# Seven-product scheme for the first feed-forward too, with in-place weight sums and quartered conditioning weights, in a one-core decoder step

## What is computed

```
c -> s1, sc1, g1, s2, sc2, g2, s3, sc3, g3 = silu(c) @ w_ada + b_ada      # w_ada: 1024 x 9216
h = x + 0.5 * g1 * swiglu(modulate(x, g_ffn1, s1, sc1), w1_gate, w1_up, w1_down)
n = modulate(h, g_mix, s2, sc2); z = n @ w_in
h = h + g2 * (mix of a convolution branch and a sparse attention branch, from z) @ w_out
h = h + 0.5 * g3 * swiglu(modulate(h, g_ffn2, s3, sc3), w2_gate, w2_up, w2_down)
y = rmsnorm(h, g_final)
def swiglu(h, wg, wu, wd): return (silu(h @ wg) * (h @ wu)) @ wd
```

## Time and profile before

| | us |
|---|---|
| median of 3 runs | 2677.19 |
| lowest and highest | 2675.59, 2679.48 |
| the profiled execution's own time | 2673.52 |
| its span in the trace | 2671.7 |
| PE busy | 2509.7 (94%) |
| POOL busy | 1202.6 (45%) |
| DVE busy | 1401.6 (52%) |
| ACT busy | 605.1 (23%) |

### The profile page before, as it was taken

The page is one execution under the profiler, slowest core; times in us unless marked ns, Lnnn a source line. Parts: engine busy times, 40 slices in busy tenths (PEclk is TensorE's granted clock), DMA queues, the critical chain, the costliest instruction groups (busy, mean ns, idle before and its releaser), DMA issues.

```text
span 2671.7 us, 42548 instructions
## 1 busy us (share of the span) xinstructions
PE 2509.7 (94%) x15750; PEld 2331.9 (87%) x15750; DVE 1401.6 (52%) x2533; ACT 605.1 (23%) x1094; POOL 1202.6 (45%) x862
## 2 busy tenths in 40 slices
PE   4999999999999888899999769999899999999998
PEld 2999999999999766699998436789799999999997
DVE  5333333333333727799998645452574444444444
ACT  3311011110102313312344357410511111111113
POOL 1232323223333325546999020124057777777774
PEclk8999999999999879999999879999999999999999
DMA  8322222222211432231224600234011111111112
GB/s 284 119 72 79 71 79 76 67 77 79 72 50 56 148 82 73 73 105 48 83 86 169 196 7 1 77 117 144 1 41 54 48 47 47 47 47 47 47 48 81
DMA packets 208660, 209.94 MB, mean 79 GB/s; under 512 B 14143, under 2 KB 161715, under 8 KB 207657
## 3 DMA queue, kind: packets, MB, share of 16 engines
q1 hardware_dynamic: 198380, 181.70, 21.8%
q10 hardware_dynamic: 10181, 26.90, 3.1%
HBM read 173.03 MB, written 28.94 MB: 76 GB/s over the span
## 4 chain that ended last, share of the span: by engine, by line
PE 82%; DVE 6%; issue 4%; ACT 3%; SPq 3%; DMA 1%; POOL 1%; ACTq 0%; DVEq 0%; POOLq 0%
PE main L249 16%; PE main L250 16%; PE main L251 16%; PE main L2243 4%; PE main L2244 4%; PE main L2245 4%; PE main L2333 2%; PE main L2334 2%; PE main L2335 2%; SPq L1472 2%; DVE pick L1287 2%; PE main L1692 1%; PE aux L2243 1%; PE aux L2244 1%; PE aux L2245 1%
## 5 line engine op out<-in xcount | busy, mean ns | idle before, releaser
L249 PE MATMUL main<-nhi,whi 128*128 128x352 f32 (+1 forms) x2136 | 698.5, 327 | 15.6 <-DVE nlo L465 14.2
L250 PE MATMUL main<-nlo,whi 128*128 128x352 f32 (+1 forms) x2136 | 688.0, 322 | 0.0
L251 PE MATMUL main<-nhi,wlo 128*128 128x352 f32 (+1 forms) x2136 | 687.6, 322 | 0.0
L236 POOL CAST whi<-raw 128x1024 fp32r<-128x1024 f32 x119 | 127.5, 1071 | 989.1 <-PE main L251 697.0
L249 PEld LDWEIGHTS main<-nhi,whi 128*128 128x128 f32 (+1 forms) x2136 | 402.2, 188 | 45.2 <-issue 32.2
L250 PEld LDWEIGHTS main<-nlo,whi 128*128 128x128 f32 (+1 forms) x2136 | 403.0, 189 | 0.6
L251 PEld LDWEIGHTS main<-nhi,wlo 128*128 128x128 f32 (+1 forms) x2136 | 401.9, 188 | 0.6
L238 POOL TENSOR_TENSOR wlo<-raw,whi 128x1024 fp32r<-128x1024 f32 x119 | 296.7, 2493 | 9.5
L687 DVE TENSOR_TENSOR tmp<-main,tmp 128x352 f32<-128x352 f32 x66 | 34.6, 525 | 395.6 <-PE main L251 394.5
L2170 POOL TENSOR_TENSOR blo<-raw,bhi 128x512 fp32r<-128x512 f32 x152 | 203.6, 1340 | 12.2
L2243 PE MATMUL main<-nhi,bhi 128*128 128x352 f32 x576 | 188.6, 327 | 8.3 <-DVE nlo L465 4.5
(11 more groups left out here) (376 smaller groups left out, 4934.5 us busy)
## 6 DMA issues: line engine op xcount, KB each, us to landing
ada_raw<-in_w_ada SPq DMA_DIRECT2D x18, 2048.0 KB, 9.0
raw<-in_w_gate SPq DMA_DIRECT2D x44, 512.0 KB, 3.9
raw<-in_w_up SPq DMA_DIRECT2D x44, 512.0 KB, 3.8
raw<-in_w_down SPq DMA_DIRECT2D x44, 512.0 KB, 3.6
raw<-in_w_in SPq DMA_DIRECT2D x40, 512.0 KB, 3.8
gate_d<-zraw ACTq DMA_DIRECT2D x16, 528.0 KB, 2.7
gates<-gate_d SPq DMA_DIRECT2D x16, 528.0 KB, 4.8
zsw<-zraw ACTq DMA_DIRECT2D x42, 132.0 KB, 2.5
```

Of the source, the lines that this page charges most:

```text
L249: pe.matmul(bank, w_hi[:, w], hi(c), start=(i == 0), stop=False)
L250: pe.matmul(bank, w_hi[:, w], lo(c), start=False, stop=False)
L251: last = pe.matmul(bank, w_lo[:, w], hi(c), start=False, stop=(i == n - 1))
```

## The change

- Feed-forward 1 is done by the same function as feed-forward 2 (ffn, called twice, with a set of semaphore bases each: Signals). Its plain version is gone.
- The four weight sums of a matrix are made in place in the raw tiles (add), so wsum is gone. A raw tile is held until its last sum: tiles 3 and 5 of a step are loaded when the fourth sum of matrix 0 or 1 is set, a count called wsum_set.
- Blocks, units, bank order and DVE's combinations come in another order, and the tile of the second half (sub 1) is loaded first.
- A w_ada tile is loaded and multiplied in quarters of 128 columns (load_ada_part, pe_ada_part), through one buffer ada_part of 512 KB. SP issues the quarters between the raw tiles, and PE multiplies them at four places of a step, two in each matrix. The last tile's turn moves into the last downs.
- The first two tiles of w_in get split buffers of their own, and the loads of the cache pages wait for the first two products of z.

The core of the diff (the functions of the old winograd that come again unchanged in ffn are left out):

```diff
-        def ffn(q, T0, A0, wg, wu, wd, i, nrm, with_ada, by_chunk=None):
...
-            def ada_loop(sp, j):
-                g = INIT_ADA // 4 + j
-                sp.wait_ge(ada_mm, g + 2)
-                sp.dma_start(ada_raw[:, 1], L0["w_ada"].rearrange("(k p) m -> p k m", p=P)
-                             [:, :, bass.ds(g * 4 * P, 4 * P)]).then_inc(ada_in[1], 16)
...
+        def pe_ada_part(pe, g, i):
+            pe.wait_ge(ada_in[1], 16 * (INIT_ADA // 8 + 4 * (g - INIT_ADA // 4) + i + 1))
+            if i == 0:
+                pe.wait_ge(ada_out, g + 1)
+            for k in range(KD):
+                rows = slice(32 * (k % 4), 32 * (k % 4) + 32)
+                last = pe.matmul(aux[rows, 1, bass.ts(i, P)], ccol[:, NCOND * k:NCOND * k + 32], ada_part[:, k, :],
+                                 start=(k < 4), stop=(k >= 4), skip_group_check=True)
+            last.then_inc(ada_mm, 1)
+        def load_ada_part(sp, g, i):
+            sp.wait_ge(ada_mm, ada_parts(g - 1) if i == 0 else ada_parts(g, i))
+            sp.dma_start(ada_part[:, :, :], L0["w_ada"].rearrange("(k p) m -> p k m", p=P)
+                         [:, :, bass.ds(g * 4 * P + i * P, P)]).then_inc(ada_in[1], 16)
...
+        USED_BY_UNIT = (1, 3, 5, 6, 7, 8, 10, 11)
+        def ffn(q, sg, T0, wg, wu, wd, i, nrm, with_ada, banks_free, ring_free, by_chunk):
+            def load(sp, j, k, dst, src):
+                if not isinstance(j, int) and k in (3, 5):
+                    sg.wsum_set.wait(sp, 8 * j - (4 if k == 3 else 0))
+                elif not isinstance(j, int):
+                    sg.block_ready.wait(sp, blocks_at(j) + (-4, -2, 0, None, 8)[k])
...
+                with sp.Fori(1, NPAIR) as j:
+                    for k, (w, sub) in enumerate(((wg, 1), (wg, 0), (wu, 1))):
+                        load_up(sp, j, k, w, sub)
+                    part(j, 0)
+                    load_up(sp, j, 3, wu, 0)
+                    part(j, 1)
+                    for half in range(2):
+                        load_down(sp, j, half)
+                    part(j, 2)
+                    part(j, 3)
...
+                        elif k < NRING:
+                            sg.down_done.wait(pool, 24 * j - (12 if k < 3 else 0))
...
+                    for m in range(2):
+                        k0, b0, w0 = 2 * m, 8 * m, 8 * j + (4 * m - 8)
+                        a21, a22, a11, a12 = (raw_half(k0 + tile, half) for tile in range(2) for half in range(2))
+                        pool.wait_ge(raw_ready[k0 % RING], 16 * (2 * j + raw_turn(T0 + k0)))
+                        block(b0, a21)
+                        block(b0 + 1, a22)
+                        s1_set = add(w0, 1, a22, a21, a22, ALU.add, b0 + 2, 0)
+                        pool.wait_ge(raw_ready[(k0 + 1) % RING], 16 * (2 * j + raw_turn(T0 + k0 + 1)))
+                        block(b0 + 2, a11)
+                        s1_set()
+                        block(b0 + 3, a22)
+                        s2_set = add(w0, 2, a22, a22, a11, ALU.subtract, b0 + 4, 1)
+                        s2_set()
+                        block(b0 + 4, a22)
+                        s3_set = add(w0, 3, a11, a11, a21, ALU.subtract, b0 + 4, 2)
+                        s3_set()
+                        block(b0 + 5, a11)
+                        block(b0 + 6, a12)
+                        s4_set = add(w0, 4, a12, a12, a22, ALU.subtract, b0 + 7, 3)
+                        s4_set()
+                        block(b0 + 7, a12)
...
+            def pe_up(pe, j):
+                for m in range(2):
+                    f, c, a, e, d, b = (G_BANKS, U_BANKS)[m]
+                    s = block(0)
+                    pe_unit(pe, s, Q[0], bank(f), True, False)
+                    s = block(1)
+                    pe_unit(pe, s, T4, bank(c), True, False)
+                    pe_unit(pe, s, Q[1], bank(f), False, True)
+                    s = block(2)
+                    pe_unit(pe, s, B11, bank(a), True, False)
+                    pe_unit(pe, s, Q[0], bank(e), True, False)
+                    pe_part(pe, j, 2 * m)
+                    s = block(3)
+                    pe_unit(pe, s, T1, bank(d), True, False)
+                    s = block(4)
+                    pe_unit(pe, s, T2, bank(b), True, True)
+                    s = block(5)
+                    pe_unit(pe, s, T3, bank(c), False, True)
+                    s = block(6)
+                    pe_unit(pe, s, B21, bank(a), False, True)
+                    pe_unit(pe, s, Q[1], bank(e), False, True)
+                    pe_part(pe, j, 2 * m + 1)
+                    s = block(7)
+                    pe_unit(pe, s, B22, bank(d), False, True)
...
+                comb(6, SX, unit[:, SX, :], bank(b), units=18)
+                comb(7, C21, unit[:, SX, :], bank(c), units=19, after=6)
+                comb(8, C22, unit[:, C21, :], unit[:, C22, :], ALU.subtract, after=7)
+                comb(9, C22, unit[:, C22, :], bank(d), after=8)
+                prod(2, C21, unit[:, C21, :], 2, S21)
+                prod(3, C22, unit[:, C22, :], 3, S22)
+                hidden_lo(dve, j, 1, C21, 1, 0)
+                prod(4, S11, bank(a), 4, S11)
+                hidden_lo(dve, j, 2, C22, 1, 1)
+                prod(5, SQ0, bank(e), 5, SQ0)
+                hidden_lo(dve, j, 3, S11, 0, 0)
...
+            sp.wait_ge(acc_done, ACC_Z + 6)
```

More of the change, by code:

```diff
@@ new lines, in pe @@
+                pe_downs(pe, 0)
+                sg.xlo_done.wait(pe, 4)
+                with pe.Fori(1, NPAIR - 1) as j:
+                    pe_up(pe, j)
+                    pe_downs(pe, j)
+                j = NPAIR - 1
+                pe_up(pe, j)
+                sg.block_ready.wait(pe, NBLOCKS)
+                for d in range(24):
+                    t, c = d // 8, d % 8
+                    if c == 0:
+                        sg.hlo_done.wait(pe, 6 * j + (4, 6, 6)[t])
+                    pe_down(pe, j, True, d, c // 4, t, c % 4)
+                    by_chunk["pe"](pe, d)
@@ new lines, in pe, with hidden_hi, spread @@
+                by_chunk["pe_end"](pe)
+            SUB_T0 = [(sub, t) for sub in range(2) for t in range(NTC)]
+            SUB_T = [(1, 2), (1, 0), (1, 1), (0, 0), (0, 2), (0, 1)]
+            xsum, spare = xa_f[:, 2], xb_f[:, 2]
+            def hidden_hi(act, j, n, slot, sub, t):
+                sg.prod_done.wait(act, 6 * j + n + 1)
+                act.activation(hid_hi[:, sub, tcs(t)], unit[:, slot, :], ACT.Copy).then_inc(sg.hhi_done.sem, 1)
+            def spread(act, n, dst, src):
+                sg.xsum_done.wait(act, n)
+                act.activation(dst, src, ACT.Copy).then_inc(sg.xhi_done.sem, 1)
@@ L696, in dve_down @@
+            def dve_down(dve, j, last, d, t, c, before):
+                order = LAST_ORDER if last else ORDER
+                out = bank(order[d % len(order)])
                 n = TC if t < 2 else PLAST
-                dve.wait_ge(acc_done, A0 + 36 * j + 12 + d + 1)
-                ffn_wait(dve, q, "down_free", 24 * j + before + 1)
+                sg.down_done.wait(dve, 24 * j + d + 1)
+                if not is_first(j):
+                    sg.drained.wait(dve, 24 * j - 24 + before + 1)
@@ new lines, in dve @@
+            def dve(dve):
+                dve_first(dve)
+                dve_downs(dve, 0, lambda d: x_steps(dve, 5) if d == 3 else None)
+                with dve.Fori(1, NPAIR - 1) as j:
+                    dve_up(dve, j)
+                    dve_downs(dve, j)
+                j = NPAIR - 1
+                by_chunk["dve_start"](dve)
+                dve_up(dve, j)
+                for d in range(24):
+                    t, c = d // 8, d % 8
+                    dve_down(dve, j, True, d, t, c, 12 * (c // 4) + 4 * t + c % 4)
+                    by_chunk["dve"](dve, d)
+                by_chunk["dve_end"](dve)
```

997 lines of the change are left out of this document (404 added, 593 removed).

## The result

The changed kernel takes 2792.96 us (median of 4 runs, 2787.55 to 2799.76), the kernel before beside it 2678.34 us: a ratio of 1.0428, interval 1.0397 to 1.0460. It is slower, as forecast, and inside the range of 2715 to 2795 us, but only by 2 us, and 35 us above the 2758 us that I had predicted; two of its four runs lie above the range. The profiled execution takes 2797.43 us with a span of 2795.6 us, 123.9 us more than before.

The account below looks back on a forecast made before the run. The prediction took PE to bound both feed-forward loops. It summed 68.5 + 5 + 8 = 81.5 us onto the profiled 2673.5 us, giving 2755 us, or 2758 us for the median, with a range of 2715 to 2795 us.

Parts of the forecast that it names:

- The mechanism of feed-forward 1: Steps 1 to 10: third w_ada quarter, queued behind the second down tile, stops PE 7.3 us; with clock loss, +68.5 us.
- +0.8 us a step, +8 us in ten steps: Feed-forward 2, end of matrix 1: DVE's splits late beside POOL, PE's wait 1.3 us instead of 0.5 us.
- the sign: What the changed profile would show in feed-forward 2: steps of 66 to 67 us, with the hid_lo wait grown.
- gaps of POOL: Feed-forward 2: part of DVE's 1.5 us lateness falls into POOL's gaps, so PE's wait was taken as 1.3 us.
- The clock behind that wait: Feed-forward 2, PE's clock after the wait for DVE's splits: the forecast put no loss on it.
- the third rival: Feed-forward 2: two more DVE tail operations wait for POOL, 1.0 us each; 2778 us, chance 0.15.
- The sum: Whole kernel: 68.5 + 5 + 8 = 81.5 us more on the profiled execution's 2673.5 us.
- the two first steps: First step of each feed-forward: DVE delayed by ACT's copy, 2 us each; with gained quarter products and rounding, +5 us together.
- The rest: all 0: Between feed-forward 1 and z, page loads and z's own buffers: no change in time, 0 us.
- The quarter comes in time: Feed-forward 1: third w_ada quarter lands before PE wants it, -28 us there; 2662 us, chance 0.06.
- The wait without the clock: Feed-forward 1: PE pauses but the granted clock holds, 23 us less; 2735 us, chance 0.15.
- DVE's tail is longer: Feed-forward 2: two more operations of each step's tail wait for POOL, 1.0 us each; 2778 us, chance 0.15.

Follow-up runs that it names:

- E5: Changed kernel with 42 unused matmuls before the third quarter's product in steps 1 to 10 of feed-forward 1, filling PE's pause: 2784.52 us, ratio 1.0405.
- E1: Changed kernel with SP issuing the third w_ada quarter ahead of the second down tile: 2710.63 us, ratio 1.0118.
- E7: Changed kernel with the third w_ada quarter issued ahead of the second down tile and DVE's and the downs' orders refitted: 2675.32 us, ratio 0.9974.
- E8: Changed kernel with POOL held from splitting the second down tile until DVE has made the step's last hid_lo: 2786.52 us, ratio 1.0389.
- E9: E7's kernel with PE, in each feed-forward's last step, waiting for down blocks one tile at a time, not all at once: 2656.25 us, ratio 0.9915.
- E4: Kernel before the change, with only the cache page loads made to wait for the first two products of z: 2682.65 us, ratio 1.0003.
- E2: Changed kernel with DVE making both hid parts of token chunk 0 before the product and split for chunk 1: 2827.51 us, ratio 1.0555.
- E6: Changed kernel with DVE making C21, S11, SQ0, C22, C12 (C12 in slot SX) and downs taking chunks 0, 2, 1: 2761.42 us, ratio 1.0300.
- E3: Changed kernel with the edits of E1 and E2 together: 2740.11 us, ratio 1.0223.

## Why the prediction was right, and where it was not

- **The mechanism of feed-forward 1: right, and shown.** The forecast had PE wanting the third quarter 32.1 us after the downs' end, and it wanted it at 32.3 (236.03 to 268.28). It had the quarter there at 39.4; it came at 40.0. Inside that, errors offset each other: POOL's chain took 34.2 us, not 33.3 (a block that needs the sum just before it begins some 1.50 us after that sum, not 1.36), SP issued the quarter 0.78 us after the sum, not 0.17, since the down tile goes first, and the quarter landed in 4.74 us, nearer the lower bound of 3.9, not in 5.6. The pause is 7.8 us for 7.3, the clock 2.0 us (by E5 1.9, 2.1 on the mean) for 2.3, the step 79.0 (79.3 on the mean) for 78.5. E1 shows that the place in SP's queue is the cause, E7 that without any wait the step is 2.8 us shorter than before.
- **Feed-forward 2: the term that was mis-sized.** The step "+0.8 us a step, +8 us in ten steps" measured 2.8 us a step on the mean of nine (65.7 to 68.4, where the sign was to be 66 to 67), and +33.5 us with the first and last steps. What makes DVE late was right in kind: POOL works beside it at the end of matrix 1. The wait was mis-sized, 2.0 us for the forecast's 1.3. DVE's tail ahead of the first down is 7.4 us (2193.33 to 2200.70) for the forecast's 7.2, and that nearness is luck: undisturbed its ten operations would take about 4.7 us and not 5.5, since they follow one another at 0.43 to 0.56 us; the splits lost 1.7 us, as forecast; and the two unit by unit products lost another 1.0 us, which the forecast left out, since it put them at 0.54 us by the earlier trace rows. That row is a mean over the old order. The 0.2 us that the forecast took off for gaps of POOL was not there, PE starts 0.23 us behind the split, and its units ahead of it take 5.6 us.
- **The clock behind that wait** was put at nothing. At the 1.3 us that the forecast had, this would have been right: after 1.37 us (E8) and 1.66 us (E1) the clock stayed at 1.00. At 2.0 us it fell in six of nine steps, about 1.0 us each. So a wait that was 0.7 us too short in the forecast hid a second cost. The last step adds 4.8 us; PE waits there 3.7 us for POOL's blo, 0.6 us before, which the forecast didn't have and E9 removes.
- Of the rule in the Trainium skill (SBUF — State Buffer, section Who interferes with whom), E8's rows and the trace agree with both sides: DVE operations with two SBUF inputs took up to 1.6 us beside POOL and 0.5 us without it, and the one with an input from PSUM stayed at 0.51 us at 2199.11 while POOL worked. The trace agrees on who starts first too: the split at 2198.68, 0.19 us ahead of POOL's subtraction, kept its 0.51 us. So what such an operation costs depends on the order of starts, and a mean such as the 536 ns of the earlier trace rows, the argument against the third rival, says little of another order.
- **The sum.** On the profiled execution 123.9 us came for 81.5: ten steps of feed-forward 1 some 76.9 for 68.5, ten of feed-forward 2 some 29.7 for 8, the two first steps 3.9 and 3.8 for 5 together, the rest 9.7 for 0. All four miss to the same side. That the median still fell inside the range, by 2 us where runs differ by 10, is partly luck.
- **"The rest: all 0"** missed 6.3 us between the feed-forwards and 3.4 us before the first product. The first is partly open (E4), the second lies within the start's own spread (last section).
- **The rivals.** "The quarter comes in time" was made by E1 instead of by chance: 2710.6 us, not 2662, because feed-forward 2 lost 33 us and not 8, and the wait for hid_lo then showed in feed-forward 1 as well (70.8 us a step for 68.9); with both gone (E7, E9) the kernel comes out at 2675 and 2656 us. "The wait without the clock" was made by E5 and is worth 21 us in the steps, for 23 predicted. "DVE's tail is longer", with a chance of 0.15, had the products' share as its mechanism and 28 us for feed-forward 2, near the 29.7 that came, but of other parts: it put 1.0 us on each of two operations, where two together lost 1.0 us, and it had neither the clock nor the last step.

## What to carry to other kernels

A load that nothing depends on yet is still late if it stands in a queue behind one that waits: read the order of each queue against what the loads ahead of it wait for, and move the early need forward. At the end of a step, the order in which a producer makes the parts has to be read against the order in which the consumer wants all of them; moving the first part forward (E2) only moved the wait to the second group, and refitting both orders (E6) removed it although DVE's list took as long. And a pause of PE is not paid by its own length alone: price the clock where the rows show that a pause of about that length lowered it. Here 1.7 us cost nothing more and 2.0 us often did, so an error of 0.7 us in a wait changed what it cost.

## What was not expected of the hardware

- After a rest of PE of 1.37 us the granted clock stayed at 1.00 in all nine steps of feed-forward 2 (E8), after 1.66 us in all nine of feed-forward 1 (E1). After 2.01 us it fell in six of nine, as to 0.71 and 0.86 over 8 us, and stayed at 1.00 in three (the changed kernel), after 3.25 us it fell in eight of nine, in the one shown to 0.50 for 4 us (E2). One rest of 1.79 us lowered it as well (E3, at 212.91). What decides between the two after the same rest in the same code was not tried.
- A DVE operation with two SBUF inputs that started under a subtraction of POOL ended 0.38 to 0.39 us behind it, in the changed kernel, E6 and E8; one that started just ahead of it kept 0.51 us and made POOL's longer (1.44 to 1.60 us for 1.29).
- The start of the program has a spread of its own. None of the experiments changes the code up to the first main product, yet the profiled executions of all eleven kernels reach it at 63.9 to 66.1 us in six traces, at 69.5 in one and at 73.0 to 74.6 in four. From 30 to 40 us the granted clock is 0.87 to 1.00 in the six, 0.71 in the one and 0.67 in the four. The stretches from 30 to 50 us, of E7:

```profile
30.00:40.00 10.00, 8.09 (x50) 2.07 (x42) 4.85 (x3) 4.05 (x5) 0.00 (x0) 0.67 0.35 113
40.00:50.00 10.00, 8.09 (x46) 3.23 (x42) 6.28 (x5) 2.77 (x4) 0.00 (x0) 0.67 0.59 204
```

and of E9:

```profile
30.00:40.00 10.00, 8.09 (x64) 2.86 (x56) 7.62 (x5) 4.51 (x6) 0.00 (x0) 0.94 0.61 212
40.00:50.00 10.00, 6.87 (x59) 3.35 (x62) 5.78 (x5) 3.81 (x6) 0.56 (x1) 1.00 0.97 310
```

PE is as busy in the first ten us, but at a granted clock of 0.67 instead of 0.94; in E7 it is at 0.67 until 70 us, and the first main product comes 10.7 us later. Whether the clock is the cause of that or goes with it, no run separates. Runs of one kernel also lie about 10 us apart (E9 at 2654 to 2656 and 2663 to 2668, the changed kernel at 2788 and 2797 to 2800); that the start is the cause there too is only likely, and what decides its clock was not tried. A difference of a few us between medians can be this alone, so the steps' own lengths are the better witness.
